# First attention and pooling set between the units of w_in and of w_o, with w_in's columns in another order

## What is computed

```python
h = rms_norm(x, pre_mix_g)                  # 256 x 2048
z = h @ w_in                                # 2048 x 4096: columns q, k, v, u, 1024 each
scores = einsum(q, k) / sqrt(128)           # 8 heads of 128, in chunks of 64 tokens
scores = scores + rel_bias[...]             # by clipped distance
scores = where(valid, scores, -1e30)
a = softmax(scores) @ v
p = multiscale_pool(u, pool_w, pool_scale)  # window means (2, 4, 8, 16) minus token, then 4 maps 256 x 256
m = concatenate([a, p]) @ w_o               # 2048 x 2048
x = x + rms_norm(m, post_mix_g)
```

## Time and profile before

| | us |
|---|---|
| median of 3 runs (2397.99 to 2405.3) | 2402.33 |
| the profiled execution | 2398.49 |
| its span, first to last instruction | 2396.7 |
| TensorE busy | 2267.3 (95%) |
| VectorE busy | 1503.2 (63%) |
| ScalarE busy | 1096.0 (46%) |
| GpSimd busy | 37.3 (2%) |

### The profile page before, as it was taken

One profiled execution on the slowest core, in us unless ns is written; L12 is line 12 of the kernel. 1 busy time (PEld: TensorE's weight loads), 2 busy tenths in 40 slices (PEclk: granted clock), 3 DMA queues, 4 the chain that ended last, 5 costly groups with the idle time before them and its releaser, 6 DMA issues.

```text
span 2396.7 us, 40839 instructions
## 1 busy us (share of the span) xinstructions
PE 2267.3 (95%) x15678; PEld 1916.5 (80%) x15678; DVE 1503.2 (63%) x2072; ACT 1096.0 (46%) x1542; POOL 37.3 (2%) x43
## 2 busy tenths in 40 slices
PE   7997889999999999997999999999889899999996
PEld 6886768888888888886888778888567788888885
DVE  6555458885588757876873897722465544566654
ACT  5444455444444434445455565422333534456533
POOL 0003000000000000000000000000010000000000
PEclk9999999999999999998999999999979999999998
DMA  7663445665566556554565556400335355544551
GB/s 234 191 195 120 132 149 154 189 192 184 184 184 186 186 186 186 184 164 136 181 196 159 163 155 193 151 9 11 109 107 179 114 184 193 185 149 142 162 177 65
DMA packets 389217, 378.77 MB, mean 158 GB/s; under 512 B 33954, under 2 KB 387618, under 8 KB 388258
## 3 DMA queue, kind: packets, MB, share of 16 engines
q1 hardware_dynamic: 389090, 377.00, 50.5%
HBM read 370.65 MB, written 6.29 MB: 157 GB/s over the span
## 4 chain that ended last, share of the span: by engine, by line
PE 88%; DVE 7%; ACT 2%; issue 2%; DMA 0%; POOL 0%; SPq 0%; DVEq 0%; ACTq 0%; POOLq 0%
PE acc L649 46%; PE acc L650 23%; PE acc L918 3%; PE aux L918 3%; PE acc L673 2%; PE acc L1037 1%; PE acc L1038 1%; PE acc L1039 1%; DVE w_lo L1667 1%; PE acc L674 1%; PE aux L732 1%; PE aux L870 1%; PE aux L836 1%; PE aux L1049 1%; ACT w_hi L1127 1%
## 5 line engine op out<-in xcount | busy, mean ns | idle before, releaser
L1667 DVE TENSOR_TENSOR w_lo<-raw_w,w_hi 128x1024 fp32r<-128x1024 f32 (+1 forms) x592 | 704.6, 1208 | 530.7 <-ACT w_hi L1127 529.1
L1127 ACT ACTIVATE w_hi<-raw_w 128x1024 fp32r<-128x1024 f32 (+1 forms) x592 | 615.3, 1047 | 777.4 <-PE acc L650 692.2
L649 PE MATMUL acc<-h,w_hi 128*128 128x512 f32 x1856 | 652.2, 397 | 17.7 <-DVE w_lo L1667 16.5
L650 PE MATMUL acc<-h,w_lo 128*128 128x256 f32 x1856 | 518.5, 279 | 0.0
L649 PEld LDWEIGHTS acc<-h,w_hi 128*128 128x128 f32 x1856 | 349.2, 188 | 102.9 <-issue 16.8
L650 PEld LDWEIGHTS acc<-h,w_lo 128*128 128x128 f32 x1856 | 350.2, 189 | 0.0
L649 PE MATMUL acc<-x_split,w_hi 128*128 128x512 f32 x704 | 252.8, 402 | 1.7 <-DVE k_shared L1724 1.7
L649 PE MATMUL acc<-ff,w_hi 128*128 128x512 f32 x704 | 249.1, 399 | 2.3 <-DVE ff L1889 2.3
L650 PE MATMUL acc<-ff,w_lo 128*128 128x256 f32 x704 | 197.4, 280 | 0.0
L650 PE MATMUL acc<-x_split,w_lo 128*128 128x256 f32 x704 | 196.8, 279 | 0.0
L649 PE MATMUL acc<-xs_b,w_hi 128*128 128x512 f32 x512 | 182.6, 401 | 1.3 <-DVE w_lo L2082 0.8
(11 more groups left out here) (319 smaller groups left out, 3259.3 us busy)
## 6 DMA issues: line engine op xcount, KB each, us to landing
raw_w<-in_w_up SPq DMA_DIRECT2D x176, 512.0 KB, 3.5
raw_w<-in_a_w_in SPq DMA_DIRECT2D x128, 512.0 KB, 3.5
raw_w<-in_w_in SPq DMA_DIRECT2D x64, 512.0 KB, 3.7
raw_w<-in_w_down SPq DMA_DIRECT2D x64, 512.0 KB, 3.4
raw_w<-in_b_w_qg SPq DMA_DIRECT2D x64, 512.0 KB, 3.7
raw_w<-in_w_o SPq DMA_DIRECT2D x32, 512.0 KB, 3.5
raw_w<-in_a_w_out SPq DMA_DIRECT2D x32, 512.0 KB, 3.5
raw_w<-in_w_k_shared SPq DMA_DIRECT2D x32, 512.0 KB, 3.5
```

Of the source, the lines that this page charges most:

```text
L649: pe.matmul(out, wh, op[:, kt, :, :].rearrange("p h t -> p (h t)"), start=first, stop=False)
L650: mm = pe.matmul(out[:, 0:T], wl, op[:, kt, 0, :], start=False, stop=last)
L1127: act.activation(WHI[:, u % 4, 0:ku, :], RAWW[:, u, 0:ku, :], ACT.Copy).then_inc(hi_made, 1)
L1667: dve.tensor_tensor(WLO[:, u, 0:ku, :], RAWW[:, u, 0:ku, :], WHI[:, u % 4, 0:ku, :].bitcast(F32), ALU.subtract)\
```

## The change

- w_in is computed in the order u (16 units, first body by depth), v (16 units), then q and k (32 units), two heads of q, then the same two of k. v has its tokens as output rows (`token_rows`, as w_v_shared has later in the program): ScalarE takes it out of PSUM straight into `VTOK` (`v_out`), scaled by a column `RC` of 1/rms for each token. `RC` comes from two transposes of `RSTD1` after u.
- GpSimd starts with the end of u. After the pooling it adds bias and mask for each head into `BIAS` (16 adds of 128 x 256). `BIAS` lies where the heads' part of w_o's operand comes to lie, and `RC`, `SS` and `PT` lie where the loaded bias `TOEP` lay, which is why ScalarE waits for `bias_ready` before it writes `RC`.
- q is not scaled any more; VectorE scales the scores by `RC` times 1/sqrt(128) and adds `BIAS` in one instruction for each half. The second product of the scores and the flipping matrix are gone.
- Attention and pooling have no stage: each step stands after a unit n of the last 32 of w_in (n = 0 to 31) or the first 8 of w_o (n = 32 to 39), by the tables `SCORES_AT`, `PAIR_AT` and `MIX_AT`. A head's transposes stand two units after its scores, its product with v four after. Maps and heads share the banks of `AUX`, one for `turn` and one for `pv` and the maps.
- w_o's first body runs by depth, the rows of the pooling ahead of those of the heads. The gemm of w_o follows as before.

```diff
+            with ExitStack() as s2:
+                BIAS = sb(s2, "bias", [P, 8, 2, T])
...
+                TOEP = sb(s2, "bias_toeplitz", [P, 8, 384])
+            with ExitStack() as s2:
                 SS = sb(s2, "scores", [P, 2, 2, T])
                 PT = sb(s2, "probs_t", [P, 2, 384])
                 ST = sb(s2, "softmax_stats", [P, 2, 4])
+                RC = sb(s2, "rstd_columns", [P, 4])
+                sb(s2, "place_of_toeplitz", [P, 1024 + 256 - 12])
+                BAND = sb(s2, "band", [P, 2, T])
...
+        SCORES_AT = [12, 13, 20, 21, 28, 29, 33, 33]
+        PAIR_AT = [7, 11, 15, 19, 23, 27, 31, 34]
+        MIX_AT = [1, 2, 4, 5, 7, 8, 10, 11]
+        DEPTH_W_O = (2, 3, 0, 1)
+
+        def heads_at(n, table, later=0):
+
+            return [h_ for h_, at_ in enumerate(table) if at_ + later == n]
...
+            weights(2, lambda i, b: (w_in, i * 512 + (3 * HALF + b * 256)), by_depth=512)
...
+            for dst, src in ((INVC[:, :, :], h["consts"][:, CCOL["invcount"]:CCOL["invcount"] + 4 * T].rearrange("p (g t) -> p g t", g=4)),
+                             (TOEP[:, :, :], h["bias_rows"]),
+                             (BAND[:, :, :], h["consts"][:, band0:band0 + 2 * T].rearrange("p (q t) -> p q t", q=2))):
...
+            for i in range(2):
+                weights(1, lambda i_, b: (w_in, 2 * HALF + i * 512 + b * 256), by_depth=512)
...
+            for n in range(32):
+                unit_rows(n, w_in, n % 4, n // 4 % 2 * HALF + n // 8 * 256)
+            for n in range(8):
+                unit_rows(n, h["w_o"][0], DEPTH_W_O[n // 2], n % 2 * 256)
...
-            pool.wait_ge(z_ready, 16)
-            U = Z[:, 3 * HT:4 * HT, :]
+            pool.wait_ge(z_ready, 4)
...
+            for n in range(8):
+                for q in range(2):
+                    b = pool.tensor_tensor(BIAS[:, n, q, :], TOEP[:, n, (1 - q) * P:(1 - q) * P + T], BAND[:, q, :], ALU.add)
+                b.then_inc(bias_ready, 1)
...
-            gemm(8, A1, quarters(operand, 1), between=x_squares)
-
-
-            pe.wait_ge(acc_free, 4 + 32)
-            pe.wait_ge(z_ready, 16)
-            for b in range(4):
-                for j in range(4):
-                    hd, kt = 2 * b + j // 2, j % 2
-                    mm = pe.transpose(AUX[b][:, j * P:(j + 1) * P], Z[:, 2 * HT + hd, kt * P:(kt + 1) * P], IDENT)
-                mm.then_inc(v_turned, 1)
+            base = [g_ for g_ in quarters(operand, 1) for _ in range(2)]
+            first_body(A1, base, after={5: x_squares, 6: lambda: gather(AUX[0], MS1)})
+            gemm(1, A1, [])
+            pe.wait_ge(rstd_ready, 1)
+            for t_ in range(2):
+                mm = pe.transpose(AUX[1][:, t_ * P:(t_ + 1) * P], RSTD1[:, t_ * P:(t_ + 1) * P], IDENT)
+            mm.then_inc(rc_turned, 1)
+            token_rows(A1, 2)
+
...
             def scores(n):
-                pe.wait_ge(sc_free, seen(sc_free))
+                pe.wait_ge(z_ready, 4 + n // 2 + 1)
...
                 for q in range(2):
-                    out = AUX[n % 2][:, q * T:(q + 1) * T]
-                    pe.matmul(out, Z[:, n, q * P:(q + 1) * P], Z[:, HT + n, :], start=True, stop=False)
-                    mm = pe.matmul(out, FLIP[:, :], HANK[:, n, (1 - q) * P:(1 - q) * P + T], start=False, stop=True)
+                    mm = pe.matmul(AUX[n % 2][:, q * T:(q + 1) * T], ZQ[:, n, q * P:(q + 1) * P], ZK[:, n, :], start=True, stop=True)
                 mm.then_inc(scored, 1)
...
             def pv(n):
-                if n == 7:
-                    pe.wait_ge(pt_ready, seen(pt_ready))
-                if n >= 2:
-                    pe.wait_ge(mix_ready, seen(mix_ready))
-                out = ACC[n % 2]
+                pe.wait_ge(pt_ready, n + 1)
+                if n == 0:
+                    pe.wait_ge(pool_mix_ready, 8)
+                    pe.wait_ge(acc_free, 4 + 8 + 4)
+                elif n < 7:
+                    pe.wait_ge(mix_ready, n)
+                out = AUX[1 if n == 7 else 3]
...
-            pe.wait_ge(side, 4 * 16)
...
+            def beside_unit(n):
+                for h_ in heads_at(n, MIX_AT):
+                    pool_mix(h_)
+                for h_ in heads_at(n, SCORES_AT):
+                    scores(h_)
+                for h_ in heads_at(n, SCORES_AT, 2):
+                    turn(h_)
+                for h_ in heads_at(n, SCORES_AT, 4):
+                    pv(h_)
+            for n in range(32):
+                pe.wait_ge(lo_made, seen(lo_made))
+                unit(A1, n // 4 % 2, n % 4, n % 8)
+                beside_unit(n)
+            gemm(4, B1, [], side=sum_of(SQY, AUX[0], ready=sq_ready),
+                 first=lambda: first_body(B1, [(pool_mix_ready, 8)] * 4 + [(mix_ready, 2 * n + 2) for n in range(4)], depth=DEPTH_W_O,
+                                          after={n: (lambda n=n: beside_unit(32 + n)) for n in range(8)}))
...
-            pend = gemm(2, spread(), keep=True, ahead=True)
-            pend = gemm(6, copier(), pending=pend, keep=True)
+            split(1)
+            pend = gemm(2, spread(), keep=True, by_depth=True, written_out=True)
...
+            act.wait_ge(rc_turned, 1)
+            act.wait_ge(bias_ready, 8)
+            for t_ in range(2):
+                act.activation(RC[:, t_:t_ + 1], AUX[1][:, t_ * P:t_ * P + 1], ACT.Copy)
+                c = act.activation(RC[:, 2 + t_:3 + t_], AUX[1][:, t_ * P:t_ * P + 1], ACT.Copy, scale=HEAD_SCALE)
+            c.then_inc(rc_ready, 1)
+            act.wait_ge(rc_ready, 1)
+            split(1)
+            split(0, between=lambda: v_out(0))
+            split(1)
...
+            for n in range(32 + 8):
+                if n == 3:
+                    v_out(1)
+                elif n in PAIR_AT:
+                    act.wait_ge(unit_done, seen(unit_done, 4, "tile"))
+                    seen(acc_free, 2, "tile")
+                    low_out(PAIR_AT.index(n) % 2 * 2)
+                split_unit(n % 8)
+                for h_ in heads_at(n, MIX_AT, 3):
+                    pool_hi(h_)
+                for h_ in heads_at(n, SCORES_AT, 2):
+                    exps(h_)
+                for h_ in heads_at(n, SCORES_AT, 4):
+                    turned_out(h_)
+                for h_ in heads_at(n, SCORES_AT, 6):
+                    mix_head_hi(h_)
...
-            pend = gemm(2, spread(HEAD_SCALE, 0), keep=True, ahead=True, between=lambda: partial(AUX[0], MS1))
-            pend = gemm(6, spread(1.0, 8), pending=pend, keep=True)
-            split(0, between=pend)
-
-
-            dve.wait_ge(side, 4 * 16)
+            split(1)
+            partial(AUX[0], MS1)
+            pend = gemm(2, spread(), keep=True, by_depth=True)
+            for i in range(2):
+                split(0, between=None if i else pend)
+                split(1)
+                seen(unit_done, 8, "tile")
+                seen(acc_free, 2, "tile")
...
+            def pair_out(p_):
+                seen(unit_done, 4, "tile")
+                seen(acc_free, 2, "tile")
+                z = (ZQ, ZK)[p_ % 2][:, p_ // 2 * 2:p_ // 2 * 2 + 2, :]
+                join(z, p_ % 2 * 2)
+                if p_ % 2:
+                    dve.wait_ge(acc_free, seen(acc_free, 0, "tile"))
+                    dve.tensor_tensor(z, z, RSTD1[:, :].unsqueeze(1).broadcast_to([P, 2, T]), ALU.mult).then_inc(z_ready, 1)
...
-                s = dve.tensor_tensor(SS[:, n % 2, :, :], AUX[n % 2][:, :].rearrange("p (q t) -> p q t", q=2), BAND[:, :, :], ALU.add)
-                s.then_inc(sc_free, 1)
-                dve.wait_ge(sc_free, 2 + n + 1)
+                for q in range(2):
+                    b = dve.scalar_tensor_tensor(SS[:, n % 2, q, :], AUX[n % 2][:, q * T:(q + 1) * T], RC[:, 2 + q:3 + q], BIAS[:, n, q, :],
+                                                 ALU.mult, ALU.add)
+                b.then_inc(sc_read, 1)
...
-            pend = gemm(4, joiner(Y), keep=True, ahead=True)
...
+            for n in range(32 + 8):
+                if n in PAIR_AT:
+                    pair_out(PAIR_AT.index(n))
+                split_unit(n % 8)
+                for h_ in heads_at(n, MIX_AT, 3):
+                    pool_lo(h_)
+                for h_ in heads_at(n, SCORES_AT, 2):
+                    softmax_max(h_)
+                for h_ in heads_at(n, SCORES_AT, 3):
+                    softmax_norm(h_)
+                for h_ in heads_at(n, SCORES_AT, 6):
+                    mix_head_lo(h_)
+            pend = gemm(4, joiner(Y), keep=True, by_depth=True)
```

More of the change, by code:

```diff
@@ L655, in pairs_of, with first_body @@
                 return [(sem_, base + p_ + 1) for p_ in range(8)]
-            def first_body(op, gates, after={}):
-                for q in range(4):
+            def first_body(op, gates, after={}, depth=(0, 1, 2, 3), between=None):
+                for x, q in enumerate(depth):
                     for pr in range(2):
-                        pe.wait_ge(*gates[2 * q + pr])
```

(13 more changed lines are left out.)

226 lines of the change are left out of this document (97 added, 129 removed).

## The result

Twelve runs of each kernel: the kernel before 2401.82 us (2394.41 to 2405.3), the changed kernel 2406.50 us (2401.67 to 2415.33). The ratio is 1.0030, with a 95% interval of 1.0016 to 1.0045: slower by 3.8 to 10.8 us. The forecast was 2412, its range 2397 to 2422.

What follows compares the result with a forecast made beforehand. Matmuls bound most of the kernel, but attention and pooling were an engine-to-engine chain of 57.4 us. Removing it, with the costs put elsewhere, summed to +9.8 us on 2402.3: 2412 us, range 2397 to 2422.

Steps and rivals of the forecast that it cites:

- a unit or more of slack: Other PSUM banks, weights and the pooling's single bank were claimed to be free in time, costing nothing.
- the stage goes: The separate attention and pooling stretch between w_in and w_o disappears: -57.4 us.
- its matmuls between units: Attention and pooling matmuls, with two RSTD1 transposes, now stand on TensorE's own line: +22.4 us.
- v by tokens: Sixteen units of v with tokens as output rows take 2.71 us each instead of 2.76: -0.8 us.
- wait for the biases: In v, TensorE waits for weight splits held up behind ScalarE's wait for GpSimd's pooling and adds: +28.1 us (27.3 to 30.0).
- low clock behind it: After the long bias wait in v, TensorE runs at a low clock for a while: +2.3 us.
- waits before the transposes: TensorE waits for the softmax, 2.2 and 0.4 us per pair, 2.2 for heads 6 and 7: +10.0 us (5 to 14).
- clock falls at them: Clock falls at the 2.2 us transpose waits, about 2.1 us each, half of three taken: +3.1 us (0 to 8).
- turn to w_o: Banks 2 and 3 come free late at the start of w_o, behind a fold on ScalarE: +0.9 us (0 to 1.5).
- pace up to w_up: 40 units beside fp32 products may run at either of two matmul paces: 0 to +2.3 us, 1.2 taken.
- near which of two rows a wait lies: Whether 2.2 us transpose waits act like the 1.57 us idle (full pace) or the 2.30 one (clock 0.54).
- The rival on the other side: Biases ready before ScalarE's wait in v, so no TensorE time lost: -20.6 us, 2381.7 us; chance 0.10.

Runs made afterwards that it cites:

- adds first: Changed kernel with the sixteen bias adds ahead of the pooling on GpSimd, ScalarE's wait kept: 2377.28 us, ratio 0.9919.
- adds twice: Changed kernel with all sixteen bias adds on GpSimd done a second time before the biases are handed over: 2415.43 us, ratio 1.0077.
- normalise first: Changed kernel with VectorE dividing a head before it takes the next head's maximum: 2409.32 us, ratio 1.0050.

## The waits that the forecast missed

Where splits and evacuations alternate, ScalarE and VectorE empty the first pair of banks ahead of the fourth split of the next run of units. The forecast took banks to have a unit or more of slack. They have it, except behind a body taken by depth. There both pairs of banks are finished within its last unit, the first half a unit before the end, and the next body wants it as soon as the last unit is done. I moved that evacuation one split forward, on both engines:

```diff
-            def split(b, ku=KU, between=None):
+            def split(b, ku=KU, between=None, at=3):
...
-                    if q == 3 and between is not None:
+                    if q == at and between is not None:
...
-                    split(0, ku, between=lambda: out(0, 0, 7))
+                    split(0, ku, between=lambda: out(0, 0, 7), at=2)
```

> The changed kernel, but in every run of units whose splits and evacuations alternate, the last evacuation of the run before stands ahead of the third of the next run's first four splits and not of the fourth, on ScalarE and VectorE. Theory (the first bank pair is wanted half a unit after the run's last unit but one, about 1.4 us, and is emptied 2.8 us after it because a split of 1.2 us stands ahead): the waits for the banks at the second body of u (1.3 us) and of w_o (1.8 us), and the like ones at later gemms (1.2 to 1.7), shrink to 0.3 or less, and the kernel is 3 to 6 us faster than the changed one: 2400 to 2404 us, ratio 0.998 to 1.001. Rival (the split that now stands behind is wanted as soon as the bank was): the same waits under the name of the split, no gain, 2406 us.

Measured: 2401.17 us (2395.14 to 2408.22, 11 runs), ratio 1.0009 (0.9991 to 1.0028), about 5 us less than the changed kernel, again with overlapping intervals. In the trace the wait at the second body of u is gone and that of w_o has shrunk:

```profile
PE acc L669 <- DVE y L1776: 0.2, 1, 0.2
```

TensorE's waits over the whole kernel add up to 125.6 us here and to 132.0, 132.4 and 133.5 in three profiles of the changed kernel: 6 to 8 us less, since the same order is used in the later stages.

**All three edits:** own bytes, later transposes, earlier evacuations.

> Three edits together on the changed kernel: the four RSTD columns have bytes of their own, so ScalarE doesn't wait for the biases; transposes a unit later for heads 0 to 5; evacuations ahead of the third split. Theory: what each takes away stands in another place of TensorE's line, so the gains add: 2377 us for the first alone, 5 less for the second, 3 to 6 less for the third, 2366 to 2369 us, ratio 0.985. Rival (the waits of the three lean on the same queues of ScalarE and VectorE, or the pace of the matmul pairs decides more than the waits): no better than the first alone, 2374 to 2380 us.

> The version with three edits (own bytes, transposes a unit later, evacuations ahead of the third split), once more and on the same chip as the one with the first edit alone. Theory: by the waits that its trace lists up to the first w_up unit, 7.6 us against 11.1 there, plus the like at the later gemms (1 to 3 us), it is 3.5 to 7 us below the first edit alone: 2369 to 2374 us, ratio 0.986 to 0.989. Rival: the 16 us between the two medians of the first timing (2361.5 against 2377.7) are real, through fewer interruptions. Second rival: no difference, both near 2375, and the first was chance of the two paces.

Measured: 2361.46 us (2357.2 to 2377.5), ratio 0.9860 (0.9823 to 0.9897), and again 2365.15 us (2360.41 to 2375.22), ratio 0.9862 (0.9836 to 0.9888). Beside the first edit alone, timed together on one chip, it is 10 us faster (2365.15 against 2374.93), more than the 3.5 to 7 I expected, though the slowest runs of the one overlap the fastest of the other. The waits listed over the whole kernel add up to 95.4 and 96.2 us against 104.3 and 105.1, 9 us less, of which 5 lie ahead of w_up and 4 behind. So the gains add; the 1 to 3 us that I had allowed for the later stages were too few.

## Two paces at one clock

The profiled run of the changed kernel was 16 us longer than that of before, though the terms in the table below give some 9. Starts of consecutive pairs of matmuls (128x512 and 128x256 columns) lie either 0.3467 or 0.3533 us apart, 1.9%, at a granted clock of 1.00 in both. The profile of before had both, which the earlier trace rows show as 579 and 567 instructions in 100 us; and the place in the program or the change itself may decide between them. I profiled both kernels again, unchanged.

> The kernel before, profiled once more. Theory (the pace of back-to-back pairs of matmuls, 0.3467 or 0.3533 us at clock 1.00, is drawn anew at interruptions and then held, and doesn't belong to a kernel or a place): the stretches at either pace lie elsewhere than in the first profile (fast 28 to 299, 322 to 345, 400 to 553 us), and the span differs from 2396.7 by a few us while the waits stay within 0.2 us. Rival (the pace belongs to the place in the program, by its addresses or transfers): the same stretches at the same paces again.

> The changed kernel, profiled once more. Theory: the pace between 120 and 620 us, which was the slow one nearly throughout, is now partly the fast one, the waits are as before (28.1 for the biases, 1.7 at the three pairs), and the span is below 2412.7 by up to 9 us. Rival (the change makes TensorE's pairs slower by where its buffers lie): slow again in the same stretches, span 2412 to 2413.

> The changed kernel a third time, as after_again: by the theory another pattern of the two paces than in both profiles before it, with the same waits.

The spans are 2389.8 us for the kernel before (2396.7 the first time), 2407.8 and 2399.3 for the changed one (2412.7). The waits at the biases were 28.1 and 28.0, at the pairs 1.7. Windows of the kernel before, profiled again:

```profile
600.00:700.00 100.00, 100.00 (x578) 1.00 0.61 189
...
900.00:1000.00 100.00, 100.00 (x579) 1.00 0.62 189
```

The changed kernel, third profile:

```profile
700.00:800.00 100.00, 100.00 (x579) 1.00 0.61 189
800.00:900.00 100.00, 99.66 (x568) 1.00 0.58 185
900.00:1000.00 100.00, 100.00 (x568) 1.00 0.61 187
```

The same program in the same stretch has 567 instructions in one execution and 579 in another, so the pace is not a property of the place. It changes at an interruption and then holds: the slow one began between 550 and 600 us in one profile of before and between 1050 and 1100 in the other, and between 800 and 900 in the last one above. Behind the first unit of w_up the two kernels run the same code; that part took 2038.1 and 2030.2 us in the profiles of before, 2040.6, 2038.5 and 2030.6 in those of the changed kernel. The scatter of 10 us lies there and belongs to neither. One part of my theory didn't hold in the second profile of the changed kernel: it was slow again from 400 to 1000 us. And one stretch looks tied to the change: from 200 to 260 us, in q and k with heads between the units, all twelve traces with attention woven in have a mean of 0.351 to 0.353 per pair, where both of before have 0.347 throughout w_in from 60 us on. What makes the pace one or the other, I can't say.

That gives a better measure than the span: the time from TensorE's first w_in matmul to its first of w_up.

| kernel | us |
|---|---|
| before | 343.4, 343.5 |
| changed | 355.4, 353.9, 353.1 (mean +10.6) |
| own bytes | 322.6, 322.6 |
| adds first | 323.9 |
| adds twice | 363.9 |
| normalise first | 357.8 |
| later transposes | 349.4 |
| earlier evacuations | 349.5 |
| all three edits | 317.4, 317.8 |

This measure is not free of chance either, because the clock fall of 1.6 us at heads 6 and 7 comes and goes in it. It is there in two of the three profiles of the changed kernel and in those of the adds first and twice, and absent in own bytes (twice), normalise first and earlier evacuations, at the same two waits. So of the 4.7 and 4.6 us that later transposes and earlier evacuations seem to gain on the mean of the changed kernel, their waits explain 2.1 and 3.0; the rest is clock and pace.

## Why the prediction was right, term by term

| term | predicted, us | measured, us |
|---|---|---|
| the stage goes | -57.4 | -57.4 |
| its matmuls between units | +22.4 | +23.4 |
| v by tokens | -0.8 | -0.7 |
| wait for the biases | +28.1 | +28.1 |
| low clock behind it | +2.3 | +2.3 (2.6, 2.6, 1.8) |
| waits before the transposes | +10.0 | +6.7 |
| clock falls at them | +3.1 | +1.1 (1.6, 1.6, 0) |
| turn to w_o | +0.9 | +0.6 |
| banks at the second bodies | none | +3.1 |
| pace up to w_up | +1.2 | about +2 |

Measured terms are means of the three profiles of the changed kernel where these differ. The pace is the excess of its pairs over 0.3467 us, 2.1 to 2.8 us in the three profiles over the pairs recorded, less the 0.6 and 0.9 that the kernel before has, with some room for records that are missing; it is an estimate.

The predicted sum is +9.8. The measured terms sum to +9.2 where the traces show +10.6 up to w_up; 1.4 us are not placed. By the ratio of the timed runs it is +7.2 (3.8 to 10.8). That the sum came this close is in part luck: the terms for softmax and clock at the heads were too high by 5.3 us together, and those for banks, matmuls and pace, one of which I had put at nothing, too low by 4.9. What was not luck is the large term, the wait for the biases.

- **The bias wait** was right in every step, since each had a row: the length of GpSimd's queue from the earlier trace rows, ScalarE's order from the code, the arrival of TensorE from the units. The adds were 0.68, taken at 0.67. The kernel with its own bytes, the one with the adds first and the one with the adds twice bear it out.
- **The matmuls** miss 1.0 us because a head's transposes cost more than the distance of their starts in the earlier trace rows; the pairs around them start late, too:

```profile
198.32 0.40 PE L669 MATMUL acc<-h,w_hi 128*128 128x512 f32 x1
...
198.80 0.55 PE L805 MATMUL aux<-consts,scores 128*128 128x128 f32 x3
199.11 0.48 PE L669 MATMUL acc<-h,w_hi 128*128 128x512 f32 x1
...
199.54 0.40 PE L669 MATMUL acc<-h,w_hi 128*128 128x512 f32 x1
```

  Two pairs with the transposes between take 1.22 us (199.54 - 198.32) where two pairs alone take 0.70, so 0.52 for a head and not 0.39. Score and pooling calls held, 0.87 for two, with the late first pair counted in.
- **The softmax chain** was sized from single rows at 2.2 and 0.4 us a pair, and measured 1.7 and none; heads 6 and 7 at 1.4 and 0.8, and measured 0.99 and 0.67. The order of the queue was right, and the reason in it half: the second maximum does stand ahead of the normalising, but taking it out of the way gained nothing.
- **The clock falls** did not come where I had looked for them, and one came where I had not. At the three pairs I had priced waits of 2.2 us, next to the 2.30 of the earlier trace rows; they were 1.7, next to the 1.57 of the earlier trace rows, and the clock held in every profile. The kernel that normalises first shows the other side, three idles of 2.4 us and three falls, at 1.5 us each where I had 2.1. But heads 6 and 7, with 0.99 and 0.67 us, have a fall in two of three profiles, and with 1.12 and 0.67 none in the third. So the length of the one idle before it doesn't tell whether the clock falls, and my question, near which of two rows a wait lies, was put too simply. What decides at heads 6 and 7 stays open.
- **"The other banks have a unit or more of slack"** was the step that failed: 3.1 us at 45.41 and 289.73. At both, a body taken by depth stands ahead, and the code has a split of 1.2 us ahead of the evacuation; the order of instructions was there to be read.
- **The rival on the other side** said what the time would be were the biases there in time: -20.6. With that wait taken away the traces give 343.5 - 322.6 = -20.9 up to w_up, and the timed runs -21 and -22.5 by their ratios. The rival was wrong as a forecast and right as a price.

## What to carry to other kernels

When work is hidden behind other work, look at what guards its memory: the change hid a chain of 35 us, and 28 came back through a wait that four columns in borrowed bytes had put ahead of an unrelated queue. For a moved helper add up its engine's whole row from the last event that starts it, and compare with the moment at which the first engine that waits gets there; above that point each microsecond is paid in full. A fraction of a per cent is better judged by the distance between two events in several traces than by spans or single runs, when the rest of the program runs at a pace that changes by itself.

## What the runs showed of the hardware that I had not expected

- Pairs of matmuls run at 0.3467 or 0.3533 us with the same granted clock, held for hundreds of us; over 500 us that is 9.5 us, more than the effect of this change.
- A GpSimd add of 128x256 starts every 0.68 us in a row of sixteen with VectorE at rest and every 1.13 beside its splits; VectorE's split grows from 1.22 to 1.75 us at the same time. I had expected the first to suffer, not both this much.
- Three fp32 transposes between pairs of matmuls cost TensorE 0.52 us where their own starts span 0.39.
- The same two short idles, 0.99 and 0.67 us with a head's transposes between and behind them, drop the clock to 1.2 GHz for some 3.4 us in one execution and not in another: 4 of the 9 profiles that have these idles show the fall, for 1.6 us. Single idles of 1.7 us at the pairs of heads did so in none of 24 cases in eight profiles, those of 2.4 us in three of three.
